# Prompt attention by pairs of heads, in row and column tiles of TensorE, with the sample caches loaded during the prompt part

## Chip, cores and metric

One core of one Trainium2 chip runs the whole program in one launch. The metric is the device time of an execution in microseconds; the time of a kernel is the median of its runs.

## The reference, cut to what matters

A one-layer streaming encoder: half a SwiGLU step, a combined projection into two attention mixers, an output projection, a second half SwiGLU step, a norm. All in float32. There are 1024 prompt rows and 8 streams of 16 sample rows with a past of 512.

```python
# mixer A, prompt: chunks of 64 queries see 8 chunks to the left and their own
sc = einsum('bcqhd,bckhd->bchqk', chunked(q), k_band) * (d ** -0.5)
sc = where(valid, sc + bias, -inf); p = softmax(sc)
o  = einsum('bchqk,bckhd->bcqhd', p, v_band)
# mixer B, prompt: the 256 best keys by an indexer score, of those of earlier and own chunks
sc = einsum('bqhd,bqkhd->bhqk', q, kg) * (d ** -0.5); p = softmax(sc); o = p @ vg
x  = x + concat(o_A, o_B) @ w_out
```

Both mixers have 8 heads of 64. The sample rows attend in the same way to cached keys and values (512 rows of 8 x 64 for each stream and mixer) and to their own 16.

## The kernel before

The phases follow each other: first SwiGLU, projection with the indexer's selection, attention (`attn_phase`, L1000 to L1581), output projection, second SwiGLU. In the matmul phases each float32 product is three passes of a high and a low part (`three_pass`, L185 to L187); in the attention the products are plain float32, which the trace shows as two matmul instructions for each call.

The prompt part of `attn_phase` goes over 16 tiles of 128 queries: `x` = 0 is mixer A (band, at most 5 blocks of 128 keys), `x` = 1 is mixer B (1 to 8 blocks; a mask `selb` is added to the scores). `blocks_of` gives the blocks: 1, 2, 3, 4, 5, 5, 5, 5 and 1 to 8. `attn_plan` writes one order of steps, and each engine goes through it in that order, one head at a time: turn g, score g+2, value g-1, with a preparation of the next tile at head 4 and the output of the last tile at head 2.

- *prep*: SP loads 128 rows of keys and queries (`rows`) from the projection in DRAM; TensorE transposes them into the one misc buffer `pm` (L1469), ScalarE copies them to `kT` (L1387) and, scaled, to `qT` (L1392). In `qT` each head has its own 128 rows, of which the other head's 64 are zero, so a score matmul contracts 128 rows of which half add nothing.
- *score* (L1502): `ps[g % 2]` (two banks) gets 128 queries x up to 1024 keys. VectorE adds the bias or mask and takes the maximum in one instruction (L1301), then negates the maximum (L1304). ScalarE takes exp with that as its bias and sums the row (L1377).
- *turn* (L1463): TensorE transposes the probabilities by units of up to 4 blocks into `pt[u % 2]`; ScalarE or VectorE copies each unit to `pT` (L1411, L1314), by a running balance of both engines' work. `pe_turn` makes unit u wait for the copy of unit u-2.
- *value* (L1521): `pT` is the stationary operand, 64 columns of `v` move, and a tile's 8 heads fill `po` with 128 queries x 512.
- *out*: VectorE takes reciprocals of the sums and scales `po` into `osb` (L1239, L1243); TensorE transposes it into `pm`; ScalarE writes `oT_hi` (L1415) and VectorE the rest, `oT_lo` (L1324).

Between its reductions VectorE does 96 half steps of the selection of the last two query tiles of mixer B (L1271, L1273), spread evenly over the blocks.

The sample part (`sample_plan`) goes over 16 items, a mixer and a stream each. For an item SP loads 1 MB of cached keys (L1170) and 1 MB of values (L1176); buffers are double. TensorE transposes the keys, computes the scores of the 8 heads in four 32-column tiles of the array (L1555), and the values in the same four tiles (L1575). These loads, and those of the bias rows and new rows (L1160, L1164), stand in SP's queue behind a wait for the last prompt value, since their buffers lie over the prompt's.

```python
            if u >= 2:
                wait_turned(pe, u - 2)
            for dst, src in blocks:
                last = pe.transpose(dst, src, ident[:])
            last.then_inc(s_t, 1)
```

Of the kernel before, what the change touches and what calls it, by code (L numbers as in the profile page):

```python
# [22 lines left out]
P = 128  # L23
# [24 lines left out]
NEG = -1.0e30  # L48
# [449 lines left out]
def wi_phase(nc, at_x, at, x_sb, xT, ident, selb, late_acc, pre, w_in, rel_bias, urel, cos, sin, cache_idx, x_mid, proj, idx_p, idx_s):  # L498
# [7 lines left out]
    with ExitStack() as ctx:  # L506
# [293 lines left out]
        def _(dve):  # L800
# [28 lines left out]
            for t in range(TOPK // P):  # L829
                e = SELB_AT[t + 1]  # L830
                dve.memset(selb[0:CHUNK, e - CHUNK:e], NEG).then_inc(s_ich, 1)
# [13 lines left out]
            def selected(t, a, w):  # L845
                dve.tensor_scalar(selb[:, SELB_AT[t]:SELB_AT[t] + w], a[:, 0:w], GONE, NEG, ALU.not_equal, ALU.mult).then_inc(s_acc, 1)
                n_acc[0] += 1
# [94 lines left out]
SHARE = 2.6  # L942


def attn_plan():


    heads = [(x, t, h) for x in range(2) for t in range(NP) for h in range(H)]
    tiles = [(x, t) for x in range(2) for t in range(NP)]
    plan = [("prep", 0, 0), ("score", 0), ("score", 1)]  # L950
    for g, (x, t, h) in enumerate(heads):
        n = tiles.index((x, t))
        if h == 4 and n + 1 < len(tiles):
            plan.append(("prep",) + tiles[n + 1])
        plan.append(("turn", g))
        if g + 2 < len(heads):
            plan.append(("score", g + 2))
        if g >= 1:
            plan.append(("value", g - 1))
        if h == 2 and n >= 1:  # L960
            plan.append(("out",) + tiles[n - 1])
    plan += [("value", len(heads) - 1), ("out",) + tiles[-1]]
    return heads, plan
# [24 lines left out]
def attn_phase(nc, at, ident, selb, acc, proj, urel, caches, oT_hi, oT_lo, outs):  # L988
# [3 lines left out]
    with ExitStack() as ctx:  # L992
# [5 lines left out]
        sc = keep("sc", [P, 3, D], F32)  # L998
# [4 lines left out]
        osb = keep("osb", [P, 2, FW], F32)  # L1003
        small = keep("small", [P, 2, 8], F32)
        sums = keep("sums", [P, 2, H], F32)
        rec = keep("rec", [P, 2, H], F32)
        flip_s = keep("flip_s", [P, H, DEC_S], F32)
        at_big = keep.at
        rows = keep("rows", [P, 2, FW], F32)
        qT = keep("qT", [P, 2, H, P], F32)  # L1010
        kT, v = [None, None], [None, None]
        kT[0], v[0] = keep("kT0", [P, HT, SEQ], F32), keep("v0", [P, NP, FW], F32)
        rel = Plan(nc, tag, keep.at)
        kT[1], v[1] = keep("kT1", [P, HT, SEQ], F32), keep("v1", [P, NP, FW], F32)
        raw = rel("raw", [P, H, NEAR], F32)
# [3 lines left out]
        smp = Plan(nc, tag, at_big)  # L1019
        kc = [smp(f"kc{i}", [P, PAST // P, FW], F32) for i in range(2)]  # L1020
        vc = [smp(f"vc{i}", [P, PAST // P, FW], F32) for i in range(2)]
# [3 lines left out]
        snT = smp("snT", [P, 2, 2, HT, P], F32)  # L1025
        late = Plan(nc, tag, at_bias)
# [5 lines left out]
        assert smp.at <= keep.at  # L1032
# [13 lines left out]
        s_s, s_mx, s_sc, s_p = sem("scores_done"), sem("max_ready"), sem("scores_ready"), sem("exp_ready")  # L1046
# [3 lines left out]
        s_kt = sem("new_keys_placed")  # L1050
# [4 lines left out]
        heads, plan = attn_plan()  # L1055
        NH = len(heads)
        NTT = 2 * NP

        units, u0 = {}, 0
        for g, (x, t, h) in enumerate(heads):  # L1060
            n = blocks_of(x, t)[1]
            units[g] = [(u0 + j, 4 * j, min(4, n - 4 * j)) for j in range(-(-n // 4))]
            u0 += len(units[g])
# [9 lines left out]

        by_dve, todo_act, todo_dve = [], 0.0, 0.0
        for g, (x, t, h) in enumerate(heads):
            n = blocks_of(x, t)[1]
            todo_act, todo_dve = todo_act + n + 2, todo_dve + SHARE * n + 2
            for _, _, nb in units[g]:
                by_dve.append(int(todo_dve < todo_act))
                if by_dve[-1]:  # L1080
                    todo_dve += nb + 1
                else:
                    todo_act += nb + 1
        by_dve += [u % 2 for u in range(len(by_dve), u0)]

        misc, m0, lo_n = {}, 0, {}
        nlo = 0
        free_at = {}
        def use(key, by_dve):
            nonlocal m0, nlo  # L1090
            misc[key] = m0
            m0 += 1
            nlo += by_dve
            lo_n[key] = nlo
        order = []
        for e in plan:
            if e[0] == "prep":
                order += [(("k",) + e[1:], 0), (("q",) + e[1:], 0)]
            elif e[0] == "out":
                order += [(("o",) + e[1:], 1)]  # L1100
        order += [((("sk", "sq")[j], x), 0) for x in range(2) for j in range(2)]
        order += [(("so", s), 1) for s in range(len(items))]
        for key, by in order:
            use(key, by)
        keys_in_order = [k for k, _ in order]

        def sc_of(g, a, b):

            return sc[:, g % 3, a:b]
# [4 lines left out]
        def both_halves(g):  # L1114

            return in_halves(ps[g % 2][:])[:, :, 0:KS // 2]
# [13 lines left out]
        def _(sp):  # L1130
            tiles = [(x, t) for x in range(2) for t in range(NP)]

            def rows_of(n):
                x, t = tiles[n]
                if n:
                    sp.wait_ge(s_mf, misc[("q",) + tiles[n - 1]] + 1)
# [6 lines left out]

            rows_of(0)

            u = urel
            sp.dma_start(raw[:], bass.AP(u.tensor, FAR, [[1, P], [6 * P, H], [1, NEAR]])).then_inc(s_bias, 16)
            values(0)
            rows_of(1)
            sp.wait_ge(s_flipped, 2)  # L1150
            values(1)
            for n in range(2, len(tiles)):
                rows_of(n)

            for dst, c, r0, r1 in outs:
                sp.dma_start(dst, proj[r0:r1, c:c + FW]).then_inc(s_out, 16)
            sp.wait_ge(s_t, units[NH - 1][-1][0] + 1)
            sp.wait_ge(s_o, NH)
            for h in range(H):
                sp.dma_start(raw_s[h * DEC_S:(h + 1) * DEC_S, :],  # L1160
                             bass.AP(u.tensor, 6 * P * h + FAR + P - DEC_S, [[1, DEC_S], [1, KS - FAR]])).then_inc(s_bias, 16)
            for x in range(2):
                for j in range(2):
                    sp.dma_start(srow[:, x, j, :], proj_v[:, NP, x * N_QKV + (1 - j) * FW:x * N_QKV + (2 - j) * FW]).then_inc(s_sr, 16)  # L1164
# [7 lines left out]
            def cached_values(s):  # L1172
                x, b = items[s]
                if s >= 2:
                    sp.wait_ge(s_o, NH + s - 1)
                sp.dma_start(vc[s % 2][:], caches[x][1][0, b].rearrange("(k p) h d -> p k (h d)", p=P)).then_inc(s_vc[s % 2], 16)  # L1176
                if s < 2:
                    sp.wait_ge(s_zero, 6)
# [3 lines left out]
            cached_keys(0)  # L1182
            for s in range(len(items)):
                if s + 1 < len(items):
                    cached_keys(s + 1)
                cached_values(s)
            sp.wait_ge(s_out, 16 * len(outs))

        @block.gpsimd
        def _(pool):  # L1190
# [7 lines left out]
            pool.memset(qT[:], 0.0).then_inc(s_zero, 1)  # L1198

# [4 lines left out]
            pool.memset(bias[CHUNK:P, :, 0:CHUNK], NEG).then_inc(s_far, 1)  # L1204
            pool.wait_ge(s_o, NH)
            pool.wait_ge(s_mf, misc[("o", 1, NP - 1)] + 1)
# [9 lines left out]
            for s, (x, b) in enumerate(items):  # L1216
                bs = slice(b * DEC_S, (b + 1) * DEC_S)
                pool.wait_ge(s_ma, misc[("sq", x)] + 1)
                if s >= 2:
                    pool.wait_ge(s_s, NH + s - 1)  # L1220
                else:
                    pool.wait_ge(s_zero, 3)
# [8 lines left out]

# [5 lines left out]
        def dve_out(dve, key, n):  # L1237

            dve.reciprocal(rec[:, n % 2, :], sums[:, n % 2, :]).then_inc(s_rc, 1)  # L1239
            dve.wait_ge(s_rc, n + 1)  # L1240
            if n >= 2:
# [525 lines left out]
```

## Time and profile before

| | |
|---|---|
| median of 3 runs | 2822.95 us (2822.76 to 2823.84) |
| profiled execution, own time | 2820.09 us |
| its span | 2818.5 us, mean granted TensorE clock 0.971 |
| TensorE busy | 2627.0 us (93%) |
| VectorE, ScalarE, GpSimd busy | 1374.0, 672.8, 155.6 us |

The times in the rows are microseconds from the start of the span. A row of the timeline is one instruction or a merged run of one kind; a busy matmul row includes the last matmul's way through the array. "PEld" is the load of the stationary operand, which overlaps matmuls. Shapes such as 128*32 behind an op are the rows and columns of the array that it uses.

### The profile page before, as it was taken

To read this page: it belongs to the slowest core of one execution; us is meant where nothing else is said; L and a number is where in the kernel's file an instruction comes from. 1 tells how busy PE (TensorE), PEld (TensorE's weight loads), DVE (VectorE), ACT (ScalarE), POOL (GpSimd) and SP (SyncE) were. 2 spreads that over 40 slices of the span, in tenths; PEclk is the share of its full clock that TensorE was granted. 3 is DMA by queue.
4 is the path that set the end of the run, shared out by engine and by line. 5 is a ranking of instruction groups with operands and counts; after the bars stand their busy time and mean duration, and the time that the engine had idled before them with its cause. 6 is when DMAs were issued, how large, how long until landed. Compare 5 with 4: busy or idle time off the path is not lost. (4 is left out here: it accounts for less than half of the span.)

```text
span 2818.5 us, 38978 instructions
## 1 busy us (share of the span) xinstructions
PE 2627.0 (93%) x15844; PEld 2389.7 (85%) x15844; DVE 1374.0 (49%) x2539; ACT 672.8 (24%) x1228; POOL 155.6 (6%) x119
## 2 busy tenths in 40 slices
PE   6999999999998999987898996787999999999997
PEld 6999999999997899976676774576999999999997
DVE  5333333333326498997676753434333333333335
ACT  4011111111103323222656553322111111111112
POOL 0000000000000111661000001000000000000000
PEclk9999999999998999998999998998999999999999
DMA  4111111111003221123100127731210011111101
GB/s 150 60 45 45 45 31 44 45 45 38 24 5 105 56 80 64 64 81 117 38 24 31 62 67 256 246 135 32 89 45 25 34 45 45 45 45 45 45 8 68
DMA packets 117276, 181.02 MB, mean 64 GB/s; under 512 B 11424, under 2 KB 75048, under 8 KB 117168
## 3 DMA queue, kind: packets, MB, share of 16 engines
q1 hardware_dynamic: 113520, 165.35, 17.9%
q0 software_dynamic: 3648, 14.16, 1.5%
q8 instruction: 76, 1.25, 0.2%
q14 instruction: 32, 0.26, 0.0%
HBM read 155.73 MB, written 31.11 MB: 66 GB/s over the span
## 5 line engine op out<-in xcount | busy, mean ns | idle before, releaser
L347 DVE TENSOR_TENSOR f_silu<-f_silu,f_pgu 128x384 f32<-128x384 f32 x132 | 73.1, 554 | 803.4 <-ACT f_silu L287 803.4
L185 PE MATMUL f_pgu<-r_T_hi,f_gh 128*128 128x384 f32 x1056 | 360.2, 341 | 16.6 <-DVE f_gl L331 10.4
L186 PE MATMUL f_pgu<-r_T_lo,f_gh 128*128 128x384 f32 x1056 | 359.3, 340 | 0.0
L187 PE MATMUL f_pgu<-r_T_hi,f_gl 128*128 128x384 f32 x1056 | 359.2, 340 | 0.0
L185 PE MATMUL f_pgu<-r_T_hi,f_uh 128*128 128x384 f32 x1056 | 357.9, 339 | 0.0
L187 PE MATMUL f_pgu<-r_T_hi,f_ul 128*128 128x384 f32 x1056 | 357.6, 339 | 0.0
L186 PE MATMUL f_pgu<-r_T_lo,f_uh 128*128 128x384 f32 x1056 | 357.6, 339 | 0.0
L368 DVE SCALAR_TENSOR_TENSOR r_x<-f_pyx,r_x 128x512 f32<-128x512 f32 x396 | 267.0, 689 | 181.7 <-PE f_pyx L187 179.5
L185 PE MATMUL f_pyx<-f_dh,f_h_hi 128*128 128x512 f32 x792 | 309.6, 391 | 0.3 <-DVE r_x L368 0.3
L186 PE MATMUL f_pyx<-f_dl,f_h_hi 128*128 128x512 f32 x792 | 309.1, 390 | 0.0
L187 PE MATMUL f_pyx<-f_dh,f_h_lo 128*128 128x512 f32 x792 | 308.5, 389 | 0.0
L287 ACT ACTIVATE f_silu<-f_pgu 128x384 f32<-128x384 f32 x132 | 64.9, 492 | 952.9 <-PE f_pgu L187 952.9
L185 PEld LDWEIGHTS f_pgu<-r_T_hi,f_gh 128*128 128x128 f32 x1056 | 199.5, 189 | 18.8 <-issue 10.8
L186 PEld LDWEIGHTS f_pgu<-r_T_lo,f_gh 128*128 128x128 f32 x1056 | 199.6, 189 | 0.8
L187 PEld LDWEIGHTS f_pgu<-r_T_hi,f_gl 128*128 128x128 f32 x1056 | 199.5, 189 | 0.0
L186 PEld LDWEIGHTS f_pgu<-r_T_lo,f_uh 128*128 128x128 f32 x1056 | 198.1, 188 | 0.0
L185 PEld LDWEIGHTS f_pgu<-r_T_hi,f_uh 128*128 128x128 f32 x1056 | 198.1, 188 | 0.0
L187 PEld LDWEIGHTS f_pgu<-r_T_hi,f_ul 128*128 128x128 f32 x1056 | 198.1, 188 | 0.0
L187 PEld LDWEIGHTS f_pyx<-f_dh,f_h_lo 128*128 128x128 f32 x792 | 149.0, 188 | 31.3
L185 PEld LDWEIGHTS f_pyx<-f_dh,f_h_hi 128*128 128x128 f32 x792 | 149.0, 188 | 31.1 <-DVE r_x L368 0.7
L186 PEld LDWEIGHTS f_pyx<-f_dl,f_h_hi 128*128 128x128 f32 x792 | 149.0, 188 | 30.0
L1521 PEld LDWEIGHTS t_po<-t_v,t_pT 128*128 128x128 f32 x1056 | 134.5, 193 | 34.6 <-DVE t_osb L1243 14.4
(232 smaller groups left out, 4383.4 us busy)
## 6 DMA issues: line engine op xcount, KB each, us to landing
f_raw_d<-in_ffn_w_down SPq DMA_DIRECT2D x22, 1024.0 KB, 5.0
f_raw_g<-in_ffn_w_gate SPq DMA_DIRECT2D x20, 1024.0 KB, 5.4
f_raw_u<-in_ffn_w_up SPq DMA_DIRECT2D x20, 1024.0 KB, 7.9
proj<-w_stage POOLq DMA_DIRECT2D x12, 1152.0 KB, 5.6
i_raw<-in_w_in SPq DMA_DIRECT2D x12, 1024.0 KB, 5.1
t_rows<-proj SPq DMA_DIRECT2D x32, 256.0 KB, 2.9
t_kc<-in_cache_a_k SPq DMA_DIRECT2D x8, 1024.0 KB, 8.2
t_vc<-in_cache_a_v SPq DMA_DIRECT2D x8, 1024.0 KB, 5.4
```

What stands on the lines that cost most here:

```text
L185: pe.matmul(out, a[0], b[0], start=first, stop=False)
L186: pe.matmul(out, a[0], b[1], start=False, stop=False)
L187: return pe.matmul(out, a[1], b[0], start=False, stop=last)
L287: act.activation(silu[:, k % 2, :], pg[k % 2][:, 0:CW], ACT.Silu).then_inc(s_silu, 1)
L347: dve.tensor_tensor(silu[:, k % 2, :], silu[:, k % 2, :], pu[k % 2][:, 0:CW], ALU.mult).then_inc(s_free, 1)
L368: dve.scalar_tensor_tensor(xs, py[k % 4][:], 0.5, xs, ALU.mult, ALU.add).then_inc(s_acc, 1)
L1521: last = pe.matmul(po[:, h * HD:(h + 1) * HD], pT[:, g % 2, j * P:(j + 1) * P], v[x][:, k0 + j, h * HD:(h + 1) * HD], start=j == 0, stop=j ...
```

## The change

A plan step is now a pair of heads (f = 0 to 3, heads 2f and 2f+1), in the order turn g, score g+2, value g.

- *Scores*: `qT` holds both heads in their natural 64 rows without zeros. Two matmuls, one from each half of the rows, write `ps[0]` and `ps[1]`. A score step waits until both reductions of the pair before it are done.
- *Negated scores*: queries are scaled by -1/8, biases and masks change sign, VectorE adds and takes the minimum, and ScalarE computes exp(-x + min). The negation instruction is gone.
- *Turn*: a pair has 2 units (up to 4 blocks) or 4, over the same two `pt` buffers. `pT` has one slot for each head of the pair.
- *Values*: `v` (64 columns) is stationary, `pT` moves (128 columns), and the heads write rows 0 to 63 and 64 to 127 of `po`, which so holds the transposed output.
- *Output*: VectorE takes the reciprocals in the turn step of the tile's last pair, GpSimd spreads them over 512 columns, TensorE transposes them ("rec"), ScalarE copies them, VectorE multiplies `po` by them. ScalarE writes `oT_hi`, GpSimd subtracts for `oT_lo`. The transposes of the output are gone.
- *Preparation*: keys after the first value step of a tile, queries after the second.
- *Memory and loads*: the buffers of cached keys and values lie over mixer A's `kT` and `v`; SP loads those of the first two items, the bias rows and the new rows once mixer A's prompt is done, ahead of the rows of tile 11.

```diff
-    for g, (x, t, h) in enumerate(heads):
-        if h == 4 and n + 1 < len(tiles):
-            plan.append(("prep",) + tiles[n + 1])
-        plan.append(("turn", g))
-        if g + 2 < len(heads):
-            plan.append(("score", g + 2))
-        if g >= 1:
-            plan.append(("value", g - 1))
+    for g, (x, t, f) in enumerate(pairs):
+        plan.append(("turn", g))
+        if g + 2 < len(pairs):
+            plan.append(("score", g + 2))
+        if f == HT - 1:
+            plan.append(("rec", n))
+        plan.append(("value", g))
+        if f == HT - 1:
+            plan.append(("norm", n))
+        if f == 0 and n:
+            plan.append(("split", n - 1))
+        if f < 2 and n + 1 < len(tiles):
+            plan.append((("prep_k", "prep_q")[f], n + 1))
...
+            for b0 in range(0, n, 4):
+                for r in range(2):
+                    units[g].append((u0, r, b0, min(4, n - b0)))
...
+            for n in range(2, NP + 3):
                 rows_of(n)
+            sp.wait_ge(s_o, FIRST_SET)
+            for s in range(2):
+                cached_keys(s)
+                cached_values(s)
+            sp.wait_ge(s_mx, NHD // 2)
...
+            for n in range(NP + 3, NTT):
+                rows_of(n)
...
+                pool.tensor_copy(recx[:], rec[:, n % 2, :].unsqueeze(2).broadcast_to([P, H, HD])).then_inc(s_rx, 1)
...
+                pool.tensor_tensor(oT_lo[:, fs, ts], osb[:].rearrange("p (f c) -> p f c", c=P),
+                                   oT_hi[:, fs, ts].bitcast(F32), ALU.subtract).then_inc(s_olo, 1)
...
+                        dve.tensor_tensor_reduce(out=sc[:, i % 4, 0:n], in0=ps[r][:, 0:n], in1=b, scale=1.0, scalar=FIRST,
+                                                 op0=ALU.add, op1=ALU.min, accum_out=small[:, i % 8:i % 8 + 1]).then_inc(s_mx, 1)
-                    dve.tensor_scalar(small[:, 1, g % 4:g % 4 + 1], small[:, 0, g % 4:g % 4 + 1], -1.0, None, ALU.mult).then_inc(s_sc, 1)
...
+                    dve.tensor_tensor(osb[:], po[:], rT, ALU.mult).then_inc(s_os, 1)
...
-                        last = pe.matmul(ps[g % 2][:, c * P:c1 * P], qT[:, (x * NP + t) % 2, h, :],
-                                         kT[x][:, h // 2, (k0 + c) * P:(k0 + c1) * P], start=True, stop=True)
+                        for r in range(2):
+                            rs = slice(r * HD, (r + 1) * HD)
+                            last = pe.matmul(ps[r][:, c * P:c1 * P], qT[rs, n % 2, f, :],
+                                             kT[x][rs, f, (k0 + c) * P:(k0 + c1) * P], start=True, stop=True)
...
-                        last = pe.matmul(po[:, h * HD:(h + 1) * HD], pT[:, g % 2, j * P:(j + 1) * P],
-                                         v[x][:, k0 + j, h * HD:(h + 1) * HD], start=j == 0, stop=j == nb - 1)
+                        for r in range(2):
+                            h = 2 * f + r
+                            last = pe.matmul(po[r * HD:(r + 1) * HD, f * P:(f + 1) * P], v[x][:, k0 + j, h * HD:(h + 1) * HD],
+                                             pT[:, r, j * P:(j + 1) * P], start=j == 0, stop=j == nb - 1)
```

## Rows read from the trace of the kernel before

**Rows 1.** Windows of the attention by stage (us; busy and count per engine, clock, DMA)

```profile
1338.00:1495.00 157.00, 140.88 (x954) 114.00 (x955) 111.85 (x280) 96.70 (x248) 0.00 (x0) 0.99 0.10 33
...
1690.00:1712.00 22.00, 12.19 (x70) 8.46 (x68) 4.13 (x7) 5.37 (x9) 5.35 (x13) 0.61 0.68 225
...
1712.00:1834.00 122.00, 91.47 (x1224) 62.39 (x1216) 52.17 (x148) 45.84 (x108) 9.79 (x42) 0.93 0.75 250
```

**Rows 2.** Timeline of VectorE: four of the 16 scalings of a tile's output

```profile
1405.43 0.69 DVE L1243 TENSOR_TENSOR t_osb<-t_po,t_rec 128x512 f32<-128x512 f32 x1
...
1501.20 0.69 DVE L1243 TENSOR_TENSOR t_osb<-t_po,t_rec 128x512 f32<-128x512 f32 x1
...
1570.49 0.69 DVE L1243 TENSOR_TENSOR t_osb<-t_po,t_rec 128x512 f32<-128x512 f32 x1
...
1689.00 0.69 DVE L1243 TENSOR_TENSOR t_osb<-t_po,t_rec 128x512 f32<-128x512 f32 x1
```

**Rows 3.** Windows of one 5-block tile and the first tile of mixer B

```profile
1430.10:1455.50 25.40, 23.53 (x166) 19.16 (x165) 19.61 (x42) 15.08 (x37) 0.00 (x0) 1.00 0.07 22
...
1501.20:1514.80 13.60, 10.62 (x55) 9.07 (x54) 7.47 (x30) 7.31 (x27) 0.00 (x0) 0.75 0.13 40
```

**Rows 4.** Timeline of 5-block heads: start, us, engine, line, op, count [idle before]

```profile
1472.65 0.82 DVE L1301 CUSTOM_DVE_ANT_0 t_sc<-t_ps,t_bias 128x640 f32<-128x640 f32 x1 [0.54 <-PE t_ps L1502]
...
1473.40 0.59 PEld L1463 LDWEIGHTS t_pt<-r_ident,t_sc 128*128 128x128 f32 x5
...
1474.07 1.25 PE L1502 MATMUL t_ps<-t_kT,t_qT 128*128 128x512 f32 x4
...
1475.04 1.20 PEld L1521 LDWEIGHTS t_po<-t_v,t_pT 128*128 128x128 f32 x10
...
1475.35 0.82 DVE L1301 CUSTOM_DVE_ANT_0 t_sc<-t_ps,t_bias 128x640 f32<-128x640 f32 x1 [0.48 <-PE t_ps L1502]
...
1476.22 0.15 DVE L1304 TENSOR_SCALAR t_small<-t_small 128x1 f32<-128x1 f32 x1
...
1476.29 1.22 DVE L1271 MAX8 t_m<-r_late_acc 128x8 f32<-128x1024 f32 x1
...
1476.40 0.83 ACT L1377 ACTIVATE t_sc<-t_sc,t_small 128x640 f32<-128x640 f32 x1 [1.07 <-DVE t_small L1304]
...
1477.23 0.74 ACT L1411 ACTIVATE t_pT<-t_pt 128x512 f32<-128x512 f32 x2
```

**Rows 5.** Timeline of an 8-block head

```profile
1675.69 1.23 DVE L1301 CUSTOM_DVE_ANT_0 t_sc<-t_ps,r_selb 128x1024 f32<-128x1024 f32 x1 [2.91 <-PE t_ps L1502]
...
1677.15 1.15 ACT L1377 ACTIVATE t_sc<-t_sc,t_small 128x1024 f32<-128x1024 f32 x1 [2.12 <-DVE t_small L1304]
...
1678.30 1.06 ACT L1411 ACTIVATE t_pT<-t_pt 128x512 f32<-128x512 f32 x2
```

**Rows 6.** Timeline of the sample part: column tiles and a switch of tile shape

```profile
1743.77 1.01 PEld L1575 LDWEIGHTS t_po<-t_vc,t_pT 128*32 128x32 f32 x32
...
1743.99 1.06 PE L1575 MATMUL t_po<-t_vc,t_pT 128*32 128x128 f32 x32
...
1766.41 0.65 PE L1555 MATMUL t_ps<-t_kTs,t_bd 128*32 128x264 f32 x8
...
1766.99 0.10 PEld L1558 LDWEIGHTS t_ps<-r_selb,t_rep 128*128 128x128 bf16 x1 [0.42 <-issue]
```

**Rows 7.** Group of instructions by line: transposes of key and query rows

```profile
L1469 PE MATMUL t_pm<-r_ident,t_rows 128*128 128x128 f32 x128 | 21.8, 296 | 32.3 <-ACT t_kT L1387 17.4 <-DMA t_rows<-proj 11.3 <-DVE r_T_lo L1324 3.6
```

**Rows 8.** Group of instructions by line: a broadcast copy on GpSimd

```profile
L1202 POOL COPY t_bias<-t_bias 128x3072 f32<-128x3072 f32 x1 | 2.7, 2742 | 13.5 <-ACT t_bias L1397 13.5
```

**Rows 9.** Timeline between the last prompt value and the first sample score

```profile
1688.77 0.20 DVE L1239 RECIPROCAL t_rec<-t_sums 128x8 f32<-128x8 f32 x1 [7.32 <-PE t_po L1521]
...
1698.62 0.71 PEld L1469 LDWEIGHTS t_pm<-r_ident,t_srow 128*128 128x128 f32 x4 [4.47 <-issue]
...
1711.17 1.10 PE L1555 MATMUL t_ps<-t_kTs,t_bd 128*32 128x264 f32 x16
```

More of the change, by code:

```diff
@@ L941 @@
 Q2 = 2 * DEC_S
-SHARE = 2.6
+SELECT_NS = 240.0
 def attn_plan():
-    heads = [(x, t, h) for x in range(2) for t in range(NP) for h in range(H)]
+    pairs = [(x, t, f) for x in range(2) for t in range(NP) for f in range(HT)]
     tiles = [(x, t) for x in range(2) for t in range(NP)]
-    plan = [("prep", 0, 0), ("score", 0), ("score", 1)]
-    for g, (x, t, h) in enumerate(heads):
+    plan = [("prep_k", 0), ("prep_q", 0), ("bias",), ("score", 0), ("score", 1)]
+    for g, (x, t, f) in enumerate(pairs):
         n = tiles.index((x, t))
-        if h == 4 and n + 1 < len(tiles):
-            plan.append(("prep",) + tiles[n + 1])
         plan.append(("turn", g))
-        if g + 2 < len(heads):
+        if g + 2 < len(pairs):
             plan.append(("score", g + 2))
-        if g >= 1:
-            plan.append(("value", g - 1))
[L960 to L963, printed above, removed]
+        if f == HT - 1:
[7 more added lines that the diff above has]
+            plan.append((("prep_k", "prep_q")[f], n + 1))
+    plan.append(("split", len(tiles) - 1))
+    return pairs, tiles, plan
 def sample_plan(n):
@@ L1053, in attn_phase @@
         s_sr = sem("sample_rows_loaded")
-        heads, plan = attn_plan()
-        NH = len(heads)
-        NTT = 2 * NP
+        pairs, tiles, plan = attn_plan()
+        NPR, NHD, NTT = len(pairs), 2 * len(pairs), len(tiles)
+        FIRST_SET = NPR // 2
         units, u0 = {}, 0
-        for g, (x, t, h) in enumerate(heads):
+        for g, (x, t, f) in enumerate(pairs):
             n = blocks_of(x, t)[1]
-            units[g] = [(u0 + j, 4 * j, min(4, n - 4 * j)) for j in range(-(-n // 4))]
-            u0 += len(units[g])
+            units[g] = []
+            for b0 in range(0, n, 4):
+                for r in range(2):
+                    units[g].append((u0, r, b0, min(4, n - b0)))
+                    u0 += 1
+        NU = u0
         items = [(x, b) for x in range(2) for b in range(DEC_B)]
@@ L1510, in _ @@
                 elif e[0] == "value":
                     g = e[1]
[L1512 removed]
+                    x, t, f = pairs[g]
+                    n = g // HT
                     k0, nb = blocks_of(x, t)
[L1514 removed]
+                    if t == 0 and f == 0:
                         pe.wait_ge(s_v[x], 16)
[L1516 to L1519 removed]
+                    if f == 0 and n:
+                        pe.wait_ge(s_os, n)
```

423 lines of the change are left out of this document (215 added, 208 removed).

## The prediction

> **What bounds the kernel now.** The windows by stage come first. The prompt part of the attention (from 1336 us, where the first scores are reduced, to 1689) has in its mixer A half TensorE busy 90% at a granted clock of 0.99, VectorE 71%, ScalarE 62%; the sample part (1712 to 1834) moves 250 GB/s [rows 1]. The start of each tile's scaling of its output cuts the 353 us: 69 us to 1405.43 for the four tiles of 1 to 4 key blocks of mixer A, 96 us for its four tiles of 5, 69 us for mixer B's tiles of 1 to 4, 119 us for its tiles of 5 to 8 [rows 2]. Windows of one tile show that the large ones are TensorE's (23.5 of 25.4 us busy) and the small ones are not (10.6 of 13.6, with the clock at 0.75) [rows 3].
>
> The timeline of one 5-block head gives the prices. Score reductions start 2.70 us apart, and TensorE fills that: 5 transposes with their loads 0.59, four score matmuls 1.25 by the row (1.07 apart, the rest is the last one's tail), ten value loads 1.20 (the load of 128 columns, 0.12, is what sets the pace of a 64-column value matmul). VectorE works 0.82 on the reduction, 0.15 on negating the maximum, 1.22 on one half step of the selection; ScalarE 0.83 on exp and 0.74 on the two copies of transposed probabilities [rows 4]. With 8 blocks the reduction takes 1.23, exp 1.15, the copies 1.06 [rows 5]. So per block n: reduction 0.14 + 0.136n, exp 0.30 + 0.107n, one copy of 4 blocks 0.5, transposes 0.118n, scores 0.215n, values 0.24n. The 5-block pair of heads costs 5.39 now, the 8-block pair 2 x 0.54 x 8 = 8.7.
>
> **The change, part by part.**
>
> *Values.* The stationary operand becomes v, 64 columns; pT streams 128 columns; two heads write the two column halves. Price from the sample part, where 32 matmuls of 128 moving columns in four 32-column tiles end in 1.06 us [rows 6]: 0.9 without the tail, so 8 instructions in 0.22 although one alone streams for 0.107 (1.07 / 10 units of 128 columns). Column tiles overlap. With two tiles, a block of two heads is 4 instructions in 0.21 to 0.24 (0.48 now); without overlap 0.43. I take 0.24.
>
> The Trainium skill, TensorE: Matmul & The Clock Gate, Part 3, says that loads run under matmuls in flight only when the row group differs. The two column tiles share their row group. By that rule a block would be 4 x (0.06 + 0.107) = 0.67, half a 128-column load and a matmul by turns, 0.43 more over 264 pair-blocks = 113 us, and the change would be slower. The trace disagrees: 32 loads span 1.01 us inside the 1.06 of their matmuls [rows 6]; I leave it 2 in 100.
>
> *Scores.* Two K=64 tiles in different row halves, into different PSUM tensors. No row here has a row tile. Bounds per pair: overlapping like the column tiles, 0.215n; one after the other, 0.43n as now. I take 0.215n, nearest to [rows 6], the only tiles in the trace.
>
> The same section of the skill gives four row tiles of 512 columns as 3.07 times faster; no run here shows that yet, and the sum by it would be the lower bound.
>
> *Switches of tile shape.* Transposes, scores and values now have three shapes. Going from 128*32 to 128*128, the next load waits 0.42 and starts 0.58 after the first of eight matmuls whose 264 columns stream in 2 x 0.22, so 0.14 is lost [rows 6]. I take 0.12 for each, three per pair; bounds 0 and 0.42.
>
> *VectorE.* The negation goes (128 x 0.15 = 19 us busy, and 0.15 out of each chain), the subtraction for oT_lo goes to GpSimd (15 x 0.69). Per pair there stay two reductions, the selection (96 half steps over 464 head-blocks, 0.207 x 1.2 = 0.25 per block and head) and a quarter of the norm and reciprocal: 0.60 + 0.77n. ScalarE: two exps, the copies, and four 0.57 operations per tile (kT, qT, the new copy of the spread reciprocals, oT_hi): 1.5 + 0.42n for n up to 4. The DVE takes 9 of 240 copies by the new balance. GpSimd's spread is 512 elements at 2.7/3072 us, under 1 us even with its start [rows 8]; with no row of a 512-element subtraction I bound it by 0.5 and 2.7, its consumer is a tile away, and it is hidden.
>
> *The new loop.* This decides the large tiles. A pair of over 4 blocks has four units of transposes but only two PSUM buffers, so the third and fourth wait for ScalarE's copies of the first two; those are queued behind exp of the next pair, as the plan puts score g+2 before turn g+1. Behind these transposes TensorE holds score g+2, behind that stand the reductions and exp g+2, and the turn is round. For n = 5: copies of the first two units 1.06, wake 0.05, one transpose 0.12, load 0.10, switch 0.12, scores 1.07, tail 0.17, wake 0.04, reductions 0.87 and 0.92 with their read-outs, hop 0.10, exp of the second head 0.83: 5.45, against 5.39 now. For n = 8 the same terms give 7.6 (8.7 now), 0.71 per block between. Each tile's four ScalarE operations lie in the loop, 2.3, and I add 0.3: 24.4, 27.2, 30.1 and, for the last tile without preparation, 31.4.
>
> So mixer A's tiles of 5 cost 96 as now. Mixer B's last four sum to 113; the stages run ahead into the next tile (now the same sum gives 126 and the rows say 119), so 108 against 119: 11 saved.
>
> *Small tiles.* No buffer is short. VectorE needs 0.60 + 0.77n. The chain over two pairs (two reductions, exp, copies, value, turn, score and hops) is about 2.0 + 1.25n, so 1.0 + 0.62n each. I take the larger with 0.4 to 0.9 for what doesn't overlap: 2.3, 2.6, 3.3, 4.1 per pair; four pairs each make 49 per mixer, 98 against 138. Part is the boundary: the transposes of keys and queries now wait for ScalarE and VectorE at the one misc buffer (TensorE idle 32.3 before them in all, 11.3 of that once for the first rows) [rows 7]. In the new plan these three uses are a pair apart.
>
> Prompt sum: 98 + 96 + 108 = 302, 51 less. TensorE then has about 4 x 66 x 0.69 + 64 x 0.7 = 227 us of work in 302, 75%; the nearest row is the 13.6 us tile with 78% busy and clock 0.75 [rows 3]. I add 6 us for stretches at half clock.
>
> *Prefetch.* Now 22.4 us pass from the last value (1688.77) to the first sample score (1711.17); the new rows are transposed from 1698.62, after their DMA [rows 9]. With all loaded: norm and bias copy 1.4, four row transposes with their copies in turn 7.2 (4 x 1.8: at half clock 4 x 0.24 with tail and hops 1.2, and a copy 0.6), two items of keys 6.4, less overlap: 14.5, so 8 less. The first two items' 4 MB no longer compete with the third's: 3 more; bounds 5 and 17, 4 MB at 250 GB/s. The loads stand on SP ahead of the rows of tile 11. They need 17 us, and that tile's keys are wanted about 19 us after their issue: 2 us, bounds 0 and 8. The output stores are issued earlier relative to the end than now. The bigger reach of the cache tiles costs nothing: rows, queries and reciprocals are placed ahead of them.
>
> The sum: -51 + 6 - 11 + 2 = -54 on the profiled execution's 2820.1 (span 2818.5), 2766; the median of the runs is 2.9 above that execution, so **2769**.
>
> **Rivals.** *The row tiles do not overlap:* 0.215n back in the loop; 46 blocks x 4 pairs x 0.215 = 40 and some 4 in the small tiles: 2813. For: no row tile in the trace. Against: column tiles do.
>
> *The clock falls for about a third of the stage:* 1.6 us of the loop and half the small chain are TensorE's and double; a third of (32 x 1.6 + 32 x 1.5), less the 6 taken, is 27: 2796. For: the 78% tile at 0.75; against: 90% tiles at 1.0 and gaps of only about 1 us per pair.
>
> *The loop is looser than I put it* (copies move to VectorE or land earlier) and VectorE's 0.60 + 0.77n sets the large tiles: about 40 less, 2729. Against: the order of ScalarE's queue is fixed.
>
> *Slower: the clock stays at half.* Then TensorE's 227 us at full clock double to 454 against 353, with the prefetch 2823 + 101 - 9 = 2915; it decides once 227 divided by the mean clock passes 353 + 9, at a clock of 0.63 (the row between the parts has 0.61 at 55% busy [rows 1]).
>
> **How the numbers follow.** Forecast 52 in 100, row tiles serial 12, partly cold 18, looser 10, half clock 6, loads not under matmuls 2. The range runs from the looser case to the serial one, 2727 to 2813; the mixed bounds of switches, prefetch and rows lie inside. A measurement of this kernel tells about 0.2% (5.6 us) from no change: faster 0.90, within 0.02, slower 0.08.
>
> **What would show it.** In the 5-block tiles reductions of one pair start 5.3 to 5.6 us after those of the last, TensorE idles before the third unit's transposes for ScalarE's copy, and the tile takes 24 to 25 us. Pairs of score matmuls in the two row halves start almost together; ten-block value groups take about 1.2. Small tiles shorten to 9 to 16 us. The first sample score comes about 14 us after the last prompt value. I am wrong if the 5-block tiles shrink clearly, if scores still take 0.43n per pair, or if the clock of the stage drops under 0.9.

## The result and the profile after

| | before | changed |
|---|---|---|
| median (range) of the runs taken together | 2823.39 us (2822.76 to 2828.52) | 2782.12 us (2779.44 to 2783.62) |
| profiled execution, own time | 2820.09 us | 2779.44 us |

The ratio is 0.9851 [0.9837, 0.9865]: faster by 41 us, within the range, where 54 was forecast. The measured 2782 lies 13 above the forecast and 14 below the rival "partly cold" (2796). First what each engine did (page of the changed kernel: busy, share, instructions):

```profile
PE 2565.1 (92%) x15844; PEld 2306.0 (83%) x15844; DVE 1343.0 (48%) x2387; ACT 668.4 (24%) x1220; POOL 183.7 (7%) x150
```

VectorE's scalings of the output cut the prompt stage as before [rows 2]:

```profile
1399.20 0.68 DVE L1339 TENSOR_TENSOR t_osb<-t_po,t_recx 128x512 f32<-128x512 f32 x1
...
1491.91 0.69 DVE L1339 TENSOR_TENSOR t_osb<-t_po,t_recx 128x512 f32<-128x512 f32 x1 [1.32 <-PE t_po L1551]
...
1552.92 0.68 DVE L1339 TENSOR_TENSOR t_osb<-t_po,t_recx 128x512 f32<-128x512 f32 x1
...
1661.22 0.69 DVE L1339 TENSOR_TENSOR t_osb<-t_po,t_recx 128x512 f32<-128x512 f32 x1 [8.27 <-PE t_po L1551]
```

| part | before | forecast | after |
|---|---|---|---|
| mixer A, tiles of 1 to 4 blocks (from 1336) | 69.4 | 49 | 63.2 |
| mixer A, four tiles of 5 | 95.8 | 96 | 92.7 |
| mixer B, tiles of 1 to 4 | 69.3 | 49 | 61.0 |
| mixer B, tiles of 5 to 8 | 118.5 | 108 | 108.3 |
| last scaling to the end of the span | 1129.5 | -11 | 1116.3 (-13.2) |

The first row starts at 1336 us in both kernels. The small tiles are the miss: 124.2 for 98. The other 6 us that the forecast booked for the clock are inside these rows. The windows (length, busy time with count for PE, PEld, DVE, ACT and POOL, then clock, DMA share, GB/s) are the whole prompt stage of the kernel before, then of the changed kernel the whole prompt stage, its first tile, and the sample part:

```profile
1336.00:1689.00 353.00, 318.51 (x2144) 258.23 (x2144) 240.84 (x578) 207.78 (x507) 1.59 (x2) 0.98 0.15 47
...
1336.00:1661.00 325.00, 260.45 (x2148) 176.64 (x2148) 213.00 (x443) 203.80 (x500) 30.21 (x33) 0.93 0.21 67
1336.00:1351.00 15.00, 12.58 (x62) 7.56 (x64) 8.95 (x35) 7.93 (x31) 2.01 (x3) 0.57 0.37 134
...
1685.00:1830.00 145.00, 113.04 (x1228) 80.53 (x1227) 57.67 (x134) 53.47 (x113) 7.69 (x33) 0.91 0.75 258
```

TensorE is busy for 58 us less, but the stage is only 28 us shorter: the rest has become waiting. With two levels of the clock (2.4 and 1.2 GHz), a mean granted clock c over t us means 2(1-c)t us at the lower one. That is 45 us of the changed kernel's prompt stage and 14 us of the one before. Below, this is called half clock.

The 5-block tile, TensorE and VectorE by the timeline (start, duration, instruction, idle time before):

```profile
1447.95 1.35 PE L1523 MATMUL t_ps<-t_kT,t_qT 64*128 64x512 f32 x8
1449.23 1.31 PE L1551 MATMUL t_po<-t_pT,t_v 128*64 128x128 f32 x20
...
1450.96 1.04 PE L1483 MATMUL t_pt<-r_ident,t_sc 128*128 128x128 f32 x8
1453.57 0.30 PE L1483 MATMUL t_pt<-r_ident,t_sc 128*128 128x128 f32 x1 [1.57 <-ACT t_pT L1424]
1454.06 0.30 PE L1483 MATMUL t_pt<-r_ident,t_sc 128*128 128x128 f32 x1 [0.19 <-ACT t_pT L1424]
1454.29 2.25 PE L1523 MATMUL t_ps<-t_kT,t_qT 64*128 64x512 f32 x8
...
1449.35 0.82 DVE L1315 CUSTOM_DVE_ANT_0 t_sc<-t_ps,t_bias 128x640 f32<-128x640 f32 x1 [1.20 <-PE t_ps L1523]
...
1456.58 0.82 DVE L1315 CUSTOM_DVE_ANT_0 t_sc<-t_ps,t_bias 128x640 f32<-128x640 f32 x1 [3.19 <-PE t_ps L1523]
...
1462.48 0.82 DVE L1315 CUSTOM_DVE_ANT_0 t_sc<-t_ps,t_bias 128x640 f32<-128x640 f32 x1 [1.86 <-PE t_ps L1523]
...
1467.87 0.82 DVE L1315 CUSTOM_DVE_ANT_0 t_sc<-t_ps,t_bias 128x640 f32<-128x640 f32 x1 [1.25 <-PE t_ps L1523]
...
1473.70 0.82 DVE L1315 CUSTOM_DVE_ANT_0 t_sc<-t_ps,t_bias 128x640 f32<-128x640 f32 x1 [1.20 <-PE t_ps L1523]
```

The third unit's transpose (1453.57) waits 1.57 us for ScalarE's copy, as the loop of the forecast has it. The next group of scores takes 2.25 instead of 1.35: the clock has fallen (1.00 granted up to 1454.2, 0.57 in the 2.8 us after), and no idle stretch of TensorE in this turn was longer than 1.57 us. This turn, with two of the tile's ScalarE operations in it (`oT_hi` and `kT`), took 7.23. The one without any (1462.48 to 1467.87) took 5.39, where the forecast had 5.45, and the tile's four turns sum to 24.4, as forecast. Over the stage the wait is the largest of TensorE's, and a wait for GpSimd comes second (groups: busy, mean ns, idle before):

```profile
L1483 PE MATMUL t_pt<-r_ident,t_sc 128*128 128x128 f32 x528 | 85.6, 289 | 39.4 <-ACT t_pT L1424 39.1
...
L1489 PE MATMUL t_pm<-r_ident,t_rows 128*128 128x128 f32 x120 | 21.0, 301 | 3.0 <-DMA t_rows<-proj 3.0
L1489 PE MATMUL t_pm<-r_ident,t_recx 128*128 128x128 f32 x64 | 10.9, 294 | 11.9 <-POOL t_recx L1216 11.8
```

The wait for GpSimd stands at a tile's end, here of a 3-block one:

```profile
1376.37 1.09 DVE L1286 MAX8 t_m<-t_acc 128x8 f32<-128x896 f32 x1
1377.38 0.18 DVE L1326 RECIPROCAL t_rec<-t_sums 128x8 f32<-128x8 f32 x1
...
1377.68 0.61 POOL L1216 COPY t_recx<-t_rec 128x512 f32<-128x512 f32 x1 [7.08 <-issue]
...
1378.35 0.66 PE L1489 MATMUL t_pm<-r_ident,t_recx 128*128 128x128 f32 x4 [1.77 <-POOL t_recx L1216]
```

VectorE's reciprocal stands behind the pair's selection steps in its queue, although ScalarE's last sum was there at 1376.27 (1376.08 and 0.19 for its read-out), before the last of these steps began. GpSimd's spread follows, and TensorE stands in front of it.

The way into the sample part, where [rows 9] had 22.4 us (1688.77 to 1711.17), is 12.3 from the flip of the biases to the first score:

```profile
1661.10 0.51 PE L1556 MATMUL t_ps<-t_raw_s,t_flip_s 128*128 128x144 f32 x2
1662.18 0.66 PE L1489 MATMUL t_pm<-r_ident,t_srow 128*128 128x128 f32 x4 [0.57 <-DVE t_bias_s L1341]
...
1673.39 1.10 PE L1581 MATMUL t_ps<-t_kTs,t_bd 128*32 128x264 f32 x16
```

### The profile page after: what moved, and what is told of

Same layout as the page of the kernel before. It is cut to its first block and busy times, and to the rows that moved or that the text cites. A ratio compares the mean times of both kernels' runs of the same rounds, so it can differ in the third digit from the quotient of the medians.

```text
span 2777.5 us, 38885 instructions
## 1 busy us (share of the span) xinstructions
PE 2565.1 (92%) x15844; PEld 2306.0 (83%) x15844; DVE 1343.0 (48%) x2387; ACT 668.4 (24%) x1220; POOL 183.7 (7%) x150
## 5 line engine op out<-in xcount | busy, mean ns | idle before, releaser
L185 PEld LDWEIGHTS f_pgu<-r_T_hi,f_gh 128*128 128x128 f32 x1056 | 199.4, 189 | 17.3 <-issue 9.3
L280 ACT ACTIVATE f_dh<-f_raw_d 128x2048 fp32r<-128x2048 f32 x22 | 42.2, 1920 | 444.1 <-PE f_pyx L187 442.7
```

Source lines behind the costliest of these rows:

```text
L185: pe.matmul(out, a[0], b[0], start=first, stop=False)
L280: act.activation(sp_d[0][:], raw_d[:], ACT.Copy).then_inc(s_whi, 1)
```

## The experiments

All times are medians beside runs of the kernel before, which had 2822 to 2824 in each group. "Half clock" is 2(1-c)t over the prompt stage, from 1336 to the last scaling, in the one profiled execution of each kernel. With c read to 0.01 it is good to some 3 us. The differences in the text are between medians; those of the rows, the reciprocal and the prefetch to the changed kernel are about as large as the intervals of the ratios, so there the trace decides.

| kernel | median us | ratio to before | half clock |
|---|---|---|---|
| changed | 2782.1 | 0.9851 [0.9837, 0.9865] | 45 |
| rows of tile 11 first | 2776.5 | 0.9840 [0.9824, 0.9857] | 45 |
| reciprocal early | 2774.1 | 0.984 [0.982, 0.986] | 32 |
| copies between the exps | 2759.1 | 0.9768 [0.9751, 0.9784] | 37 |
| both heads in the same rows | 2851.5 | 1.0081 [1.0041, 1.0120] | 127 |
| no prefetch | 2786.5 | 0.9873 [0.9854, 0.9892] | 32 |
| the three edits | 2745.9 | 0.9734 [0.9716, 0.9752] | 6 |
| filler | 2770.7 | 0.9809 [0.9793, 0.9825] | 19 |
| no selection in small tiles | 2773.5 | 0.9822 [0.9806, 0.9839] | 38 |
| copies between, all pairs | 2768.5 | 0.9808 [0.9786, 0.9829] | 31 |
| three edits and filler | 2745.4 | 0.9729 [0.9708, 0.9750] | 6 |
| values by head | 2770.6 | 0.9816 [0.9796, 0.9836] | 13 |
| no spread transposes | 2741.9 | 0.9713 [0.9693, 0.9733] | 11 |

**Rows of tile 11 ahead of the prefetch.**

```diff
-            for n in range(2, NP + 3):
+            for n in range(2, NP + 4):
```

> The changed kernel with one loop bound moved: the rows of tile 11 are loaded ahead of the caches of the first two items instead of behind them. In the changed kernel TensorE stands 3.0 us for these rows at 1516, with VectorE and ScalarE empty meanwhile. Theory A (the DMA queue is a cost of its own): 3 to 5 us less than the changed kernel's 2782.1, about 2778. Rival B: the 4 MB then stand before the rows of tile 12 instead, and nothing is won: 2781 to 2783.

5.6 less by the medians and 3 by the ratios, as theory A had it. TensorE's 3.0 us of waits for the rows are gone, and mixer B's small tiles take 56.6 instead of 61.0, but its large ones 111.2 instead of 108.3. The forecast had 2 for the delay, with 17 us for 4 MB. In the changed kernel's trace the rows are issued 15 us after those of the tile before, and most of that is the issue of the bias rows and of the new rows, which stand between them in SP's queue. These two issues take 8.70 and 2.97 beside the prefetch, and 3.58 and 1.85 in the kernel without it, so the queue and the 4 MB act together:

```profile
1496.82 0.43 SPq L1139 DMA_DIRECT2D t_rows<-proj  x1
...
1499.87 8.70 SPq L1176 DMA_DIRECT2D t_raw_s<-urel  x8
1508.62 2.97 SPq L1180 DMA_DIRECT2D t_srow<-proj  x4
1511.63 0.43 SPq L1138 DMA_DIRECT2D t_rows<-proj  x1
```

**Reciprocal ahead of the selection steps.**

```diff
+                    if g and pairs[g - 1][2] == HT - 1:
+                        m = (g - 1) // HT
+                        dve.wait_ge(s_p, 2 * g)
+                        dve.reciprocal(rec[:, m % 2, :], sums[:, m % 2, :]).then_inc(s_rc, 1)
                     done += 2 * n // P
```

> The changed kernel with the reciprocal of a tile's sums moved on VectorE: directly behind the two reductions of the next pair instead of behind the selection steps that follow them. TensorE waits 11.8 us in all for GpSimd's spread reciprocals, nearly all in the tiles of 1 to 4 blocks. Theory A (the small tiles lost their gain at this new wait): 8 to 12 us less, about 2772. Rival B (VectorE's own pace, 0.60 + 0.77n per pair, holds the small tiles anyway): 0 to 3 us less, 2779 to 2782.

8.0 less by the medians and 3 by the ratios; theory A. The tiles of 1 to 4 blocks after the first take 6.6 less. The group of spread reciprocals in this kernel's trace:

```profile
L1493 PE MATMUL t_pm<-r_ident,t_recx 128*128 128x128 f32 x64 | 10.4, 286 | 0.3 <-POOL t_recx L1216 0.2
```

The wait of 11.8 is 0.2. Not all of it came back: the transposes' wait for ScalarE's copies grew from 39.1 to 42.3, the value matmuls' for VectorE's scaling from 0.3 to 4.5.

**Copies of the first two units between the two exps** (pairs of over 4 blocks).

```diff
                     for r in range(2):
                         i = 2 * g + r
+                        if r == 1 and g >= 2 and early(g - 1):
+                            for unit in units[g - 1][0:2]:
+                                copy_unit(g - 1, *unit)
                         act.wait_ge(s_mx, i + 1)
```

> The changed kernel with ScalarE's order changed for pairs with four units: the copies of the first two units go between the two exps of the next pair instead of behind them and behind the tile's other ScalarE work. Theory A (the loop exp, copies, third and fourth unit's transposes, scores, reductions, exp sets the large tiles): its turn shortens from 5.45 to about 4.65 us at 5 blocks, and up to 2.3 us of other ScalarE work per tile leave it: 20 to 30 us less, about 2757. Rival B (VectorE's 4.5 us per pair, tile-shape switches and the clock set them): 0 to 6 us less, 2776 to 2782.

23 less, theory A. TensorE in this kernel's 5-block tile:

```profile
1429.80 1.04 PE L1493 MATMUL t_pt<-r_ident,t_sc 128*128 128x128 f32 x8
1431.17 0.30 PE L1493 MATMUL t_pt<-r_ident,t_sc 128*128 128x128 f32 x1 [0.34 <-ACT t_pT L1398]
1431.66 0.30 PE L1493 MATMUL t_pt<-r_ident,t_sc 128*128 128x128 f32 x1 [0.19 <-ACT t_pT L1398]
1431.89 1.35 PE L1533 MATMUL t_ps<-t_kT,t_qT 64*128 64x512 f32 x8
```

The wait before the third unit is 0.34 instead of 1.57. The large tiles take 84.0 and 93.8 instead of 92.7 and 108.3, which is all of the 23 us. The same engines do the same work, so it was the order in ScalarE's queue that held the large tiles.

**Both heads' scores in the same rows** (the second head is computed from the queries and keys of the first).

```diff
-                            rs = slice(r * HD, (r + 1) * HD)
+                            rs = slice(0, HD)
```

> The changed kernel with both heads' score matmuls on rows 0 to 63 (the second head's scores are computed from the first head's queries and keys, so its result is another); same instructions, same sizes, but no two row halves at work together. Theory A (row tiles overlap, and scores lie in the loop of the large tiles): 0.215 us per block and pair more in 46 x 4 pair-blocks, 40 us, and a few in the small tiles: about 2824. Rival B (TensorE idles 39 us for copies in these tiles, so the longer scores use up idle time): 10 us more, about 2792. If row tiles do not overlap: no change.

69 more, beyond both expectations. One after the other, the group of eight takes 2.42:

```profile
1445.32 2.42 PE L1523 MATMUL t_ps<-t_kT,t_qT 64*128 64x512 f32 x8
...
1452.73 3.49 PE L1523 MATMUL t_ps<-t_kT,t_qT 64*128 64x512 f32 x8
```

1.07 more for 5 blocks is 0.214 per block, the forecast's 0.215. That is 40 us over the 46 blocks of the large tiles and 4 pairs, and 17 us over the 20 blocks of the small ones. The large tiles take 54 more, the small ones 18. So the small tiles paid about their whole price, where the forecast's price of the rival "row tiles serial" (44 us) had some 4 for them. The 14 us in the large tiles beyond the price fit the clock: 127 us of this stage are at half, and the second row is the next pair's group in such a stretch, 3.49. The two were not tested apart.

**No prefetch.**

```diff
-            sp.wait_ge(s_o, FIRST_SET)
-            for s in range(2):
-                cached_keys(s)
-                cached_values(s)
...
+            sp.wait_ge(s_mx, NHD)
+            sp.wait_ge(s_o, NPR)
```

> The loads of the first two cached items and of the sample rows go back behind the last prompt value; all else as in the changed kernel. Theory A: the prefetch is worth the 10 us by which the gap from the last prompt value to the first sample score shrank (22.4 to 12.3) and 3 for the first items' bandwidth, less the 5.6 that the delayed rows of tile 11 cost: 2787 to 2790, and the start of tile 12 about 5.6 earlier than in the changed kernel. Rival B: the sample part would have been held by something else anyway, so that only the 5.6 show: 2776 to 2780.

2786.5, theory A. Against the kernel whose rows also come in time (2776.5) the prefetch is worth 10, forecast 11. Here TensorE waits 4.94 for the bias rows; for the 4.99 before the transposes of the new rows the profile names no releaser ("issue"), though the kernel waits for their DMA there, too:

```profile
1655.73 0.69 PE L1557 MATMUL t_ps<-t_raw_s,t_flip_s 128*128 128x144 f32 x2 [4.94 <-DMA t_raw_s<-urel]
1661.41 1.09 PE L1490 MATMUL t_pm<-r_ident,t_srow 128*128 128x128 f32 x4 [4.99 <-issue]
```

In the profiled executions the part behind the last scaling is 17.6 longer than in the kernel with the rows in time, and the prompt stage 7.9 shorter. Of these, 3.4 lie in the first tile, before any cached load; 4.5 lie in mixer B's large tiles, and their cause stays open.

**The three edits together.**

> Rows of tile 11 ahead of the prefetch, reciprocal ahead of the selection steps, and the copies of the first two units between the two exps, all at once on the changed kernel. Theory A: the three waits stand one behind another (a DMA wait, a tile's end, the loop of the large tiles), so the gains of 5.6, 8 and 23 add up: 2745 to 2748. Rival B: they share the same idle time or the bound passes to VectorE, whose 0.60 + 0.77n per pair is 4.45 for 5 blocks: no more than 27 in all, 2755 to 2760.

2745.9: the gains add up (5.6 + 8.0 + 23.0 = 36.6; measured 36.2; by the ratios 30 and 33). This is the version that beats both kernels, 2.7% below the one before. The tiles of 5 take 81.7 instead of 92.7, those of 5 to 8 in mixer B 93.2 instead of 108.3, the small ones 57.9 and 53.6. The whole stage:

```profile
1336.00:1622.00 286.00, 243.92 (x2146) 167.06 (x2148) 210.86 (x442) 198.58 (x500) 29.09 (x32) 0.99 0.23 74
```

**Filler on TensorE.**

```diff
+                        if pairs[g][2] and t_nb <= 4 and k == 0:
+                            fill(pe, pairs[g][2], 4)
+                        if pairs[g][2] and t_nb > 4 and k == 2:
+                            fill(pe, pairs[g][2], 8)
                         pe.wait_ge(s_p, i + 1)
```

> TensorE gets work that nobody reads while it would wait: 4 transposes of the identity ahead of the wait for exp in pairs of up to 4 blocks, 8 ahead of the third unit's transposes in longer ones, in three of every four pairs (0.12 us each at full clock, 34 us in all, less than the waits of 1.6 us they stand in). Theory A: the 47 us at half clock that the changed kernel has in this stage lie half on its path and go, 8 to 15 us less: 2767 to 2774, granted clock of the stage over 0.97. Rival B: the half clock is granted where TensorE is not awaited, so the clock rises and the time stays (2779 to 2784) or the filler delays real work and it grows by up to 10.

Theory A: 11.5 less by transposes that nobody reads:

```profile
1336.00:1653.00 317.00, 276.45 (x2434) 200.78 (x2436) 213.31 (x443) 204.23 (x500) 30.42 (x33) 0.97 0.21 69
```

Everything that the kernel computes is the same, and 286 more matmuls stand on its busiest engine. So part of the half clock was on the path. How much is less sure than the medians suggest: the profiled execution was the slowest of this kernel's four (2775.9), and its stage is only 7.8 shorter for 26 us less at half clock.

**No selection in the small tiles** (with the reciprocal early; the steps are left out, so the selection of the last tiles is incomplete).

```diff
+                if small_tile and (i, j) != (TOPK // 8 - 1, 1):
+                    return
```

> The kernel with the reciprocal ahead of the selection (2774), and the selection steps that fall on pairs of up to 4 blocks left out (the block selection of the last tiles is then incomplete); 160 of the 464 head-blocks, so some 33 half steps of 1.2 us, 40 us of VectorE. Theory A: VectorE sets the small tiles (0.60 + 0.77n per pair and its reciprocal): the eight small tiles lose 25 to 40 us, 2735 to 2750. Rival B: the chain of one pair through all engines sets them, the selection lies in VectorE's idle time: 2769 to 2774.

2773.5 against 2774.1: no difference, Rival B. VectorE's selection is not what sets the small tiles. TensorE is the busiest engine there, at 86 to 95% (three windows over mixer A's tiles of 2 to 4 blocks in this kernel). That it sets them alone is not shown:

```profile
1350.00:1365.00 15.00, 12.92 (x106) 8.24 (x108) 6.22 (x26) 12.11 (x36) 3.15 (x3) 1.00 0.11 36
1365.00:1381.00 16.00, 15.17 (x135) 10.28 (x135) 6.92 (x21) 12.80 (x32) 1.88 (x2) 1.00 0.10 34
1381.00:1397.00 16.00, 13.81 (x113) 9.71 (x111) 11.79 (x23) 10.65 (x25) 1.38 (x2) 0.89 0.10 34
```

Three tiles did shorten in this profile (those of 2 and 3 blocks of mixer A by 1.2 and 1.9, that of 2 of mixer B by 1.0), but the time as a whole doesn't show it.

**Copies between the exps for all pairs** (the three edits, with the condition of `early` always true).

> As the kernel with the three edits (2745.9), but ScalarE does the copies of the first two units between its two exps for every pair, those of up to 4 blocks too. Theory A: in the small tiles a pair's probabilities reach TensorE 0.9 us of exp earlier, of which a third shows since TensorE is busy 85% there: 3 to 8 us less, 2738 to 2743. Rival B: the second head's exp is now late by the copies and the pair after it pays that back: 2744 to 2756.

22.5 more than with long pairs only: neither expectation, and Rival B by kind. The groups of TensorE's waits:

```profile
L1565 PE MATMUL t_po<-t_pT,t_v 128*64 128x128 f32 x1056 | 74.7, 285 | 16.4 <-DVE t_osb L1343 13.0 <-DVE t_pT L1336 2.8 <-ACT t_pT L1402 0.6
L1537 PE MATMUL t_ps<-t_kT,t_qT 64*128 64x512 f32 x176 | 49.0, 641 | 12.7 <-ACT t_qT L1414 12.7
```

With the three edits alone these two show 7.8 for the scaling and 5.4 for the queries. In a short pair ScalarE reaches the early copies before their transposes are there. That it stands there, and the queries' copy and the last exp behind it, fits these waits; I did not test it by itself. Mixer B's small tiles take 66.4 instead of 53.6, mixer A's after the first 51.6 instead of 45.0.

**Three edits and filler.**

> The three edits and TensorE's filler transposes together. With the three edits the clock of the prompt stage is already 0.98, against 0.93 in the changed kernel. Theory A: the filler's 11.5 us on the changed kernel came from its half clock alone, of which little is left: 2742 to 2747. Rival B: it also holds the clock up for what follows (sample part) and the gains add: 2734 to 2738. Rival C: the wait it stood in is gone, so it delays real transposes: 2748 to 2760.

2745.4, the same. With the three edits the clock is at 0.99 already, and the filler has nothing to give back.

**Values by head.**

```diff
-                        for r in range(2):
+                        for r, j in [(r, j) for r in range(2) for j in range(c, min(c + 4, nb))]:
                             h = 2 * f + r
```

> The changed kernel with the value matmuls of up to 4 blocks issued by head, all of the one head in the one column half and then all of the other in the other, so that successive matmuls use the same columns of the array. Theory A: only different column halves overlap, so a block of two heads takes 0.43 instead of 0.24; 264 pair-blocks x 0.19 = 50 us of TensorE, three fifths of it on the path: 2782 + 30 = 2812 (2800 to 2825), and a group of 5 blocks takes 2.1 us instead of 1.31. Rival B: the pace is set by loads and issue, which stay the same: 2779 to 2786.

Both expectations missed, and the sign too: 11.6 less by the medians, 10 by the ratios. The values of 5 blocks do take longer, 1.80 (1.31 when heads alternate; 2.1 was expected by theory A):

```profile
1429.16 1.56 PEld L1550 LDWEIGHTS t_po<-t_pT,t_v 128*64 128x64 f32 x20
1429.16 1.80 PE L1550 MATMUL t_po<-t_pT,t_v 128*64 128x128 f32 x20
```

They lie where TensorE would have waited for ScalarE (28.4 instead of 39.1 of that wait), and the clock stays up:

```profile
1336.00:1652.00 316.00, 267.97 (x2150) 190.86 (x2150) 212.67 (x444) 203.42 (x500) 29.51 (x32) 0.98 0.21 68
L1523 PE MATMUL t_ps<-t_kT,t_qT 64*128 64x512 f32 x176 | 48.6, 636 | 0.1
```

The scores' mean is 636 ns, as with the filler, where the changed kernel has 712. Here are the changed kernel, the filler and this one from the first scaling to the last:

```profile
1351.00:1661.20 310.20, 248.07 (x2089) 169.18 (x2087) 204.06 (x408) 195.87 (x470) 28.19 (x30) 0.94 0.20 64
1351.20:1653.40 302.20, 264.57 (x2368) 192.41 (x2366) 204.28 (x408) 196.25 (x470) 28.23 (x30) 0.99 0.21 66
1349.20:1651.60 302.40, 257.19 (x2091) 184.16 (x2089) 204.17 (x408) 195.55 (x470) 28.20 (x30) 0.99 0.20 66
```

Two unlike edits have the clock at 0.99 and the stage 8 us shorter, with about 31 us less at half clock. That would be about 0.25 us for each, and 0.4 by the medians of the filler. But this kernel isn't a clean second test: TensorE's wait for the rows of tile 11 is 0.3 in it instead of 3.0, and that tile alone is 4.1 shorter. Whether the edit did this I did not test.

**Without the transposes of the spread reciprocals** (three edits; the outputs are scaled by the reciprocals of other rows).

```diff
-            plan.append(("rec", n))
```

> The kernel with the three edits, less the transposes of the spread reciprocals and their copy by ScalarE (the outputs are scaled by the reciprocals of other rows). Theory A: these stand on the path of every tile, 4 transposes 0.66 on TensorE, a switch of shape and 0.57 on ScalarE: 16 x 1.0 to 1.3, so 2725 to 2731. Rival B: they fit where the engines wait: 2742 to 2746.

2741.9, 4 less than with them, at the edge of what intervals of 0.2% can tell, and nearer to Rival B. In the profiled execution the stage from the first scaling on is 6 shorter. So once the wait is gone, the transposes and ScalarE's copy cost 4 to 6 us, where theory A had 16 to 21. The reciprocal and its spread stay in this kernel and are not priced by it.

## Why the prediction was right, and where it was off

The parts that make the kernel faster came out as forecast: both kinds of tiles overlap, the large tiles keep their loop, and the loads come early. The time is 13 us over the forecast, mainly because the small tiles gained 14 us where the forecast had 41.

- *Column tiles.* Right: 0.24 per block and pair was assumed, 20 matmuls of 5 blocks take 1.31, and the next group starts 1.24 after them, 0.25 per block. Their 20 loads span 1.07 us inside it. The Trainium skill (TensorE: Matmul & The Clock Gate, Part 3) has in its list of what overlaps that loads run under matmuls in flight only when the row group differs; these share it, and the trace disagrees. (That part of the Trainium skill excepts loads into a background weight buffer.) By head, without alternation, it is 1.80.
- *Row tiles.* Right: 1.35 for the eight instructions that take 2.42 in one row half.
- *The loop of the large tiles.* Right in place, close in size: 92.7 and 108.3 for 96 and 108, which includes some clock (89.6 and 105.2 with the filler). The order of the copies alone takes 9 and 15 out of them (84.0 and 93.8). The rival "looser loop" fell for this kernel. It had 40 us less by the large tiles; with the three edits they are at 81.7 and 93.2, 29 less than forecast, and the time is 2745.9 for its 2729.
- *Switch of shape.* 0.12 was assumed. The load of the next shape waits 0.17 "issue" in the trace where the matmuls run at full clock and 0.33 where they run at half. Not tested by itself.
- *Prefetch.* 11 forecast, 10 measured (13.2 between the last scaling and the end). *Rows of tile 11:* 2 forecast, 5.6 measured (3.0 as TensorE's wait), within its bounds of 0 and 8. It priced the 4 MB by themselves; in the trace the rows are issued 15 us late, 11.7 of them by the issue of the bias rows and new rows.
- *GpSimd.* The spread takes 0.61 (under 1 forecast), the subtraction 1.27 (0.5 to 2.7), and the latter is hidden.
- *The step that failed: small tiles,* "the larger with 0.4 to 0.9 for what doesn't overlap", 98 for the eight. They took 124.2. The forecast's chain had no term for the reciprocal. It placed it, its spread and its transposes by duration alone, and did not name what stands ahead of it in VectorE's queue. Of the 26 us, 6.6 are that wait (tiles after the first, reciprocal early against changed), 4.4 the rows of tile 11 (2 of it booked elsewhere), 5.8 the first tile: I gave it 9.2 of the 49, but it already took 14.6 before and takes 15.0 now (counted from 1336; from their first score matmul 16.7 and 17.3), a cost that I overlooked in the rows of before. The other 9 are spread over the tiles. By the filler 2 of them are the clock's (the small tiles after the first, 107.5 for 109.2); the rest I can't assign.
- *The clock,* booked at 6. TensorE was at half clock for 45 us instead of 14. Of these, 13 lie in the first 15 us (6 before the change), so behind them some 35 stand against 7. The filler gets 11.5 back by the medians, 8 in the trace. The rival "partly cold" had named this with 27, so it was in part true. The row that I gave against it, "gaps of only about 1 us per pair", did not hold: the gap shown is 1.57, and the clock fell right after it.
- *Smaller things.* The range starts at 2727, while the rival that it is said to start from is at 2729. The prompt's copies are 192 and not 240; the 9 by VectorE are right.
- *The sum.* 26.2 more in the small tiles less 2 booked for the rows, 3.3 less in mixer A's large tiles, 0.3 more in B's, 6 booked for the clock apart, 2.2 more saved behind the prompt: 13.0 short; the profiled executions differ by 40.7 for 54.

## What to carry to other kernels

When an instruction moves to another engine, price the queue it joins and the queue of whoever feeds it: here a 0.18 us reciprocal behind selection steps of 1.09 left TensorE waiting 11.8 us over 16 tiles, of which some 7 came back. When TensorE's work in a stage shrinks, allow for its own time growing: here its waits came with 31 us more at half clock, so that durations read at full clock summed to too little. The first thing to try is a different order of the engine that it waits for: three moved pieces of code were worth 36 us, nearly as much as the change's own 41, and 23 of them came from ScalarE's order alone. The same move in the short pairs cost 22.

## What was not expected of the hardware

- More work on TensorE came with a faster kernel, twice: 286 unread transposes (clock 0.93 to 0.97, -11.5 us), and value matmuls 0.49 us longer per 5-block pair (0.98, -11.6 us, of which up to 4 lie in the wait for tile 11's rows). The Trainium skill (TensorE: Matmul & The Clock Gate, Part 4) says that full clock does not engage for transposes, as they do not count as PE-busy in the same way. The filler consisted of transposes against the identity, and the clock rose.
- The Trainium skill (TensorE: Matmul & The Clock Gate, Part 3) has a speedup of 3.07 for four row tiles. Two row tiles of f32 gave 2.42 / 1.35 = 1.8.
- The first prompt tile ended anywhere between 1347.6 and 1355.5 us in the thirteen traces after the change. Most of this is its start: the first score fell between 1330.1 and 1338.2, and from there to the first scaling it took 15.9 to 17.5 us (20.0 with both heads in the same rows). In the kernel with the copies between the exps the profiled execution was 2770.6 while the median of its runs was 2759.1, and its first score came 4.4 us later than the changed kernel's, of which 1.0 is a longer wait for the bias rows. The first score matmuls of the changed kernel and of that one:

```profile
1333.73 0.49 PE L1523 MATMUL t_ps<-t_kT,t_qT 64*128 64x128 f32 x4 [1.16 <-issue]
...
1338.15 0.49 PE L1533 MATMUL t_ps<-t_kT,t_qT 64*128 64x128 f32 x4 [1.16 <-issue]
```
